# State products of an RWKV-7 mixer on the array's diagonal quarters, with states kept packed

## The reference

```
S_t = S_{t-1} (diag(w_t) - kk_t (kk_t*a_t)^T) + v_t k_t^T ;  y_t = S_t r_t
```

## Time and profile before

| | |
|---|---|
| median of 3 runs | 1588.71 us (1586.63 to 1590.48) |
| the profiled execution's own time | 1587.97 us |
| its span | 1586.0 us |
| mean granted TensorE clock | 0.923 |
| PE busy | 1433.5 us (90%) |
| DVE busy | 982.6 us (62%) |
| ACT busy | 661.4 us (42%) |

### The profile page before, as it was taken

One profiled execution on the slowest core, in us unless ns is written; L12 is line 12 of the kernel. 1 busy time (PEld: TensorE's weight loads), 2 busy tenths in 40 slices (PEclk: granted clock), 3 DMA queues, 4 the chain that ended last, 5 costly groups with the idle time before them and its releaser, 6 DMA issues.

```text
span 1586.0 us, 27551 instructions
## 1 busy us (share of the span) xinstructions
PE 1433.5 (90%) x10889; PEld 1282.0 (81%) x10889; DVE 982.6 (62%) x1316; ACT 661.4 (42%) x745; POOL 152.6 (10%) x117
## 2 busy tenths in 40 slices
PE   5799799688879787999997999996999999999996
PEld 3688544367868557999997998994999999999996
DVE  0565643636546536455375567575788888888786
ACT  1354123321203113443323043334677677667763
POOL 0000133000000000000363002250000000000000
PEclk9899999788968688999998999996999999999996
DMA  7565799442050322434432533352788888888882
GB/s 271 207 240 207 282 386 381 184 177 69 40 213 2 137 80 80 148 143 167 176 136 69 220 133 97 130 193 80 288 298 298 303 321 302 304 322 297 303 310 106
DMA packets 49005, 321.17 MB, mean 203 GB/s; under 512 B 6080, under 2 KB 6224, under 8 KB 19936
## 3 DMA queue, kind: packets, MB, share of 16 engines
q1 hardware_dynamic: 41760, 292.53, 50.0%
q0 software_dynamic: 7168, 27.54, 4.7%
HBM read 315.66 MB, written 4.39 MB: 202 GB/s over the span
## 4 chain that ended last, share of the span: by engine, by line
PE 70%; issue 11%; DVE 9%; ACT 4%; DMA 4%; DVEq 1%; POOL 1%; POOLq 0%; ACTq 0%; SPq 0%
PE ps L335 33%; PE ps L2449 4%; PE ps L2451 4%; PE ps L2450 4%; PE ps L1616 3%; DMA ring<-in_w_mod 2%; PE ps L2400 2%; PE ps L493 2%; PE ps L347 2%; PE ps L725 1%; ACT wexp L324 1%; PE ps L1622 1%; PE ps L1103 1%; PE ps L1064 1%; PE ps L1081 1%
## 5 line engine op out<-in xcount | busy, mean ns | idle before, releaser
L2369 DVE TENSOR_TENSOR wexp<-ring,wexp 128x2816 fp32r<-128x2816 f32 x98 | 302.9, 3091 | 65.8 <-ACT wexp L324 65.7
L324 ACT ACTIVATE wexp<-ring 128x2816 fp32r<-128x2816 f32 x98 | 250.9, 2560 | 26.8 <-PE ps L2451 26.6
L335 PE MATMUL ps<-hx_hi,wsplit 128*128 128x320 f32 x1088 | 251.5, 315 | 4.4 <-DVE hx_lo L676 2.6
L335 PEld LDWEIGHTS ps<-hx_hi,wsplit 128*128 128x128 f32 x1088 | 186.3, 191 | 12.2 <-issue 11.3
L2449 PE MATMUL ps<-wexp,xg_hi 128*128 128x352 f32 x512 | 168.4, 329 | 2.7 <-DVE xg_lo L2585 2.7
L335 PE MATMUL ps<-hx_lo,wsplit 128*128 128x320 f32 x544 | 169.8, 312 | 0.0
L2451 PE MATMUL ps<-wexp,xg_lo 128*128 128x352 f32 x512 | 165.2, 323 | 0.0
L2450 PE MATMUL ps<-wexp,xg_hi 128*128 128x352 f32 x512 | 165.0, 322 | 0.0
L324 ACT ACTIVATE wsplit<-ring 128x2048 fp32r<-128x2048 f32 (+1 forms) x60 | 120.0, 2000 | 98.8 <-PE ps L335 67.2
L335 PE MATMUL ps<-wexp,he_hi 128*128 128x256 f32 x704 | 128.6, 285 | 0.0
L314 POOL TENSOR_TENSOR wsplit<-ring,wsplit 128x2048 fp32r<-128x2048 f32 (+1 forms) x16 | 85.5, 5346 | 340.4 <-ACT wsplit L324 340.4
(11 more groups left out here) (393 smaller groups left out, 2671.6 us busy)
## 6 DMA issues: line engine op xcount, KB each, us to landing
ring<-in_exp_w SPq DMA_DIRECT2D x100, 1408.0 KB, 7.0
ring<-in_w_mod SPq DMA_DIRECT2D x48, 1024.0 KB, 7.8
ring<-in_ffn_gu SPq DMA_DIRECT2D x22, 1024.0 KB, 4.8
arena<-in_cache_k SPq DMA_DIRECT2D x64, 256.0 KB, 6.0
arena<-in_cache_v POOLq DMA_DIRECT2D x64, 256.0 KB, 5.8
ring<-in_w_in_o SPq DMA_DIRECT2D x16, 1024.0 KB, 4.7
ring<-in_w_in_e SPq DMA_DIRECT2D x13, 1024.0 KB, 4.9
ring<-in_ffn_down SPq DMA_DIRECT2D x8, 1408.0 KB, 6.0
```

The costliest lines, as they stand in the source:

```text
L324: return nc.scalar.activation(out, in_, ACT.Copy)
L335: mm = nc.tensor.matmul(out, u, v, start=first and p == 0, stop=last and p == 2)
L2369: eng.tensor_tensor(lo, ring[:, expert_slot(j), :], hi.bitcast(F32), ALU.subtract).then_inc(lo_exp, 1)
```

## The change

States stay packed in `S9`, 64 rows for each head of a pair. The block matrices `ATm` and `Sbd` and their memsets are gone. A state product takes the head's 64 rows of the state and of the chunk's matrix and writes the head's 64 partitions, so that it lies on a 64x64 quarter on the array's diagonal. Chunks are taken in pairs (`PAIRS`): (0, 1) and (2, 3) in tiles 0 and 1, and (0, 2), (1, 3), (4, 6), (5, 7) in tile 2, two chunks of a pair always in different groups of 32 rows. `pair_products` alternates the two chunks matmul by matmul, and every pair writes banks 2 to 5; one ScalarE copy of 128x1024 takes all four banks to `AC`. The decay is no longer applied to each term but once to the sum. DVE's state update is add, add, multiply, on 256 columns in tiles 0 and 1 and on two chunks at once, 512 columns, in tile 2. In tiles 0 and 1 both pairs' products now stand ahead of step 0, and the turn of the next tile stands behind the wait for the third state.

```diff
--- before.py
+++ after.py
@@ -1175,12 +1175,10 @@
     gup = aR.take(512)
     st = aR.take(5, 4 * P)
     stR, stQ, stK, stB, stV = (st[:, n, :].rearrange("p (j t) -> p j t", t=P) for n in range(5))
-    ATm = aR.take(2, 512)
+    AC = [aR.take(4, 256)]
     S9 = aR.take(9, 256)
-    Cst = aR.take(2, 256)
-    Sbd = aR.take(2, 512)
-    T1 = aR.take(256)
-    T2 = aR.take(256)
+    AC.append(aR.take(4, 256))
+    Tst = aR.take(2, 256)
     RW = aR.take(4, P)
     Y0 = aR.take(4, P)
     tokK, tokB, tokV = (aR.take(512) for _ in range(3))
@@ -1306,8 +1304,6 @@
         nc.vector.tensor_tensor(tmpR[:, :, :], kk[:, :, :], kk[:, :, :], ALU.mult
                                 ).then_inc(rp["kk_sq"], 1)
         nc.vector.memset(S9[:, 0, :], 0.0)
-        nc.vector.memset(Sbd[:, :, :], 0.0)
-        nc.vector.memset(ATm[:, :, :], 0.0)
         dve.wait_ge(rp["sig"], 1)
         flat = "p j t -> p (j t)"
         for j in range(4):
@@ -1356,21 +1352,19 @@
     def both(*names):
         return [f"{x}{h}" for x in names for h in range(2)]
 
+    PAIRS = (((0, 1), (2, 3)), ((0, 2), (1, 3), (4, 6), (5, 7)))
+
...
-        def chunk_matrices(cc):
-            dve.wait_ge(r_pe, P_.at(f"wc{cc}"))
-            x = cc % 2
-            for q in (0, 64):
-                nc.vector.tensor_copy(heads4(ATm[q:q + 64, x, :])[:, :, q:q + 64],
-                                      heads4(ps[q:q + 64, 2 + 2 * x, :])[:, :, q:q + 64])
-            for q in (0, 64):
-                last = nc.vector.tensor_tensor(
-                    Cst[q:q + 64, x, :].rearrange("p (j v) -> p j v", v=64),
-                    heads4(ps[q:q + 64, 3 + 2 * x, :])[:, :, q:q + 64],
-                    pend[q:q + 64, :, cc:cc + 1].to_broadcast([64, 4, 64]), ALU.mult)
-            last.then_inc(r_dve, 1)
-
-        def chunk_state(cc):
-            s_ = state(part, cc)
-            pe4 = pend[:, :, cc:cc + 1].to_broadcast([P, 4, 64])
-            v4 = "p o (j v) -> p (o j) v"
-            nc.vector.tensor_tensor(T1.rearrange("p (j v) -> p j v", v=64), s_.rearrange(v4, v=64),
-                                    pe4, ALU.mult)
+        def new_states(step, s_, C_, decay, ps_):
+            n = s_.shape[1]
+            tmp = Tst[:, 0:n, :]
+            nc.vector.tensor_tensor(tmp, s_, C_, ALU.add)
             dve.drain()
-            nc.vector.tensor_tensor(T1, T1, Cst[:, cc % 2, :], ALU.add)
-            dve.wait_ge(r_pe, P_.at(f"y{cc}"))
-            nc.vector.tensor_tensor(T2.rearrange("p (j v) -> p j v", v=64),
-                                    ps[:, 6, 0:256].rearrange("p (j v) -> p j v", v=64), pe4,
-                                    ALU.mult)
+            dve.wait_ge(r_pe, P_.at(f"y{step}"))
+            nc.vector.tensor_tensor(tmp, tmp, ps_, ALU.add)
             dve.drain()
-            if part == 0 and cc < C - 1:
-
-                for q in (0, 64):
-                    h = slice(q, q + 64)
-                    last = nc.vector.tensor_tensor(
-                        heads4(Sbd[h, (cc + 1) % 2, :])[:, :, q:q + 64],
-                        *(x[h, :].rearrange("p (j v) -> p j v", v=64) for x in (T1, T2)), ALU.add)
-                last.then_inc(r_dve, 1)
-            last = nc.vector.tensor_tensor(s_, T1.unsqueeze(1), T2.unsqueeze(1), ALU.add)
-            if part or cc == C - 1:
-                last.then_inc(r_dve, 1)
+            nc.vector.tensor_tensor(s_.rearrange("p x (j v) -> p x j v", v=64),
+                                    tmp.rearrange("p x (j v) -> p x j v", v=64), decay, ALU.mult
+                                    ).then_inc(r_dve, 1)
             dve.drain()
-        chunk_matrices(0)
-        chunk_matrices(1)
-        chunk_state(0)
-        for cc in range(2, C):
-            chunk_matrices(cc)
-            chunk_state(cc - 1)
-        chunk_state(C - 1)
+        for p, (ca, cb) in enumerate(PAIRS[part]):
+            dve.wait_ge(r_act, A_.at(f"ac{p}"))
+            if part:
+                decay = pend[:, :, ca:cb + 1:2].rearrange("p j x -> p x j")
+                new_states(p, S9[:, ca + 1:cb + 2:2, :], AC[p % 2][:, 1:4:2, :],
+                           decay.unsqueeze(3).to_broadcast([P, 2, 4, 64]),
+                           ps[:, 6, :].rearrange("p (x n) -> p x n", x=2))
+            else:
+                for y, cc in enumerate((ca, cb)):
+                    decay = pend[:, :, cc:cc + 1].rearrange("p j x -> p x j")
+                    new_states(cc, S9[:, 0:1, :], AC[p % 2][:, 2 * y + 1:2 * y + 2, :],
+                               decay.unsqueeze(3).to_broadcast([P, 1, 4, 64]),
+                               ps[:, 6:7, 0:256])
         dve.wait_ge(r_act, A_.at("y0"))
         nc.vector.tensor_tensor(col(yT), stg(ps[:, 7, :].rearrange("p (j t) -> p j t", t=P)),
                                 stg(Y0), ALU.add).then_inc(r_dve, 1)
@@ -1576,17 +1546,11 @@
         act.wait_ge(r_pe, P_.at("yr"))
         nc.scalar.activation(Y0[:, :, :].rearrange("p j t -> p (j t)"), ps[:, 0, :], ACT.Copy
                              ).then_inc(r_act, 1)
-        if t and part == 0:
-            act.wait_ge(r_dve, rdve[t - 1].at(f"s{n_chunks(0) - 1}"))
-        for cc in range(n_chunks(part) if part else 1):
-            if cc > 1:
-                act.wait_ge(r_pe, P_.at(f"y{cc - 2}"))
-            s_ = state(part, cc)
-            for q in (0, 64):
-                last = nc.scalar.activation(
-                    Sbd[q:q + 64, cc % 2, :].rearrange("p (o j v) -> p o j v", o=1, v=P)[:, :, :, q:q + 64],
-                    s_[q:q + 64, :, :].rearrange("p o (j v) -> p o j v", v=64), ACT.Copy)
-            last.then_inc(r_act, 1)
+        for p in range(len(PAIRS[part])):
+            act.wait_ge(r_pe, P_.at(f"wc{p}"))
+            if p >= 2:
+                act.wait_ge(r_dve, D_.at(f"s{p - 2}"))
+            nc.scalar.activation(AC[p % 2][:, :, :], ps[:, 2:6, 0:256], ACT.Copy).then_inc(r_act, 1)
 
     def turn_tensor(pe, t):
         pe.wait_ge(r_prod, t + 1)
@@ -1703,59 +1667,70 @@
                                    stop=True)
         last.then_inc(r_pe, 1)
 
-        def chunk_products(cc):
-            x = cc % 2
-            if part:
-                if cc == 0:
-                    pe.wait_ge(r_act, A_.at("masked"))
-                r = slice(RC * (cc // 2), RC * (cc // 2) + RC)
-                Bs, Ks = mats[x]["ET"], mats[x]["MT"]
-            else:
-                r = slice(RC * cc, RC * cc + RC)
-                Bs, Ks = tokB, tokK
+        def pair_products(p):
+            if p:
+                pe.wait_ge(r_act, A_.at(f"ac{p - 1}"))
+            elif part:
+                pe.wait_ge(r_act, A_.at("masked"))
             for j in range(4):
                 for n in range(3):
-                    for h in range(2):
-                        q = 64 * h
-                        own = slice(j * P + q, j * P + q + 64)
-                        U, W = (ZF[r, 2 * P * j + y + q:2 * P * j + y + q + 64] for y in (0, P))
-                        B, K, V = (y[r, own] for y in (Bs, Ks, tokV))
-                        a_, c_ = (ps[q:q + 64, y + 2 * x, own] for y in (2, 3))
-                        if n == 0:
-                            mm_(a_, W, B, start=True, stop=True)
-                        elif n == 1:
-                            mm_(c_, K, V, start=True, stop=False)
+                    for y, cc in enumerate(PAIRS[part][p]):
+                        if part:
+                            r = slice(RC * (cc // 2), RC * (cc // 2) + RC)
+                            Bs, Ks = mats[cc % 2]["ET"], mats[cc % 2]["MT"]
                         else:
-                            last = mm_(c_, B, U, start=False, stop=True)
+                            r = slice(RC * cc, RC * cc + RC)
+                            Bs, Ks = tokB, tokK
+                        for h in range(2):
+                            q = 64 * h
+                            own = slice(j * P + q, j * P + q + 64)
+                            U, W = (ZF[r, 2 * P * j + z + q:2 * P * j + z + q + 64] for z in (0, P))
+                            B, K, V = (z[r, own] for z in (Bs, Ks, tokV))
+                            a_, c_ = (ps[q:q + 64, z + 2 * y, 64 * j:64 * j + 64] for z in (2, 3))
+                            if n == 0:
+                                mm_(a_, W, B, start=True, stop=True)
+                            elif n == 1:
+                                mm_(c_, K, V, start=True, stop=False)
+                            else:
+                                last = mm_(c_, B, U, start=False, stop=True)
             last.then_inc(r_pe, 1)
 
-        def chunk_step(cc):
-            pe.wait_ge(r_dve, D_.at(f"ac{cc}"))
-            if cc:
-                pe.wait_ge(r_dve, D_.at(f"s{cc - 1}"))
-            if part or cc == 0:
-                pe.wait_ge(r_act, A_.at(f"bd{cc}"))
-            for j in range(4):
-                for q in (0, 64):
-                    mm_(ps[q:q + 64, 6, j * 64:j * 64 + 64],
```

(65 more changed lines are left out.)

## The result

The changed kernel takes 1579.57 us (median of 15 runs, 1571.64 to 1586.73) against 1589.77 (15 runs, 1586.43 to 1595.75): a ratio of 0.9924, 95% interval 0.9908 to 0.9941, so 0.76% or 12 us faster; the medians themselves lie 10.2 us apart. The forecast was 1578.3, in a range of 1565 to 1592.

The account below looks back on a forecast made before the run. TensorE, at half clock most of the time, bounds three stretches of 73.64 us, all on the path. Tiles 0 and 1 together -0.3, tile 2 -10.1, sum -10.4: 1577.6, or 1578.3 beside the median; range 1565 to 1592.

Parts of the forecast that it names:

- PE is in order: Reason why the three tile stretches are on the path: the next unit's matmuls stand right behind, so savings reach the end.
- (c): Pair products: two chunks in different 32-row groups run side by side, 1.92 us a pair at full clock, 2.76 at half.
- (a): Two memsets on DVE go; they were hidden behind a wait for ScalarE's sigmoid, so worth 0.
- (b): One ScalarE copy per pair, 1.03 us; PE waits for it between pair 0 and pair 1, a hole of 1.28 us a tile.
- B: Rival: row groups don't overlap in the pair products, which cost as now; sum +6.1 us, 1595; chance 0.16.
- (d): State products on 64x64 diagonal quarters keep the old pace: 1.05 us a chunk at full clock, 1.85 at half.
- C: Rival: two row halves in one bank take turns; each of 16 steps costs 1.6 us more, 1604; chance 0.05.
- (e): DVE's state chain, 0.93 us on 256 columns, is now exposed in tiles 0 and 1; a period is 2.97 us at half clock.
- (f): The next tile's turn now stands behind the wait for s2; the price, 1.07 us, is inside the third period of (e).
- The clock: TensorE's clock falls to 0.50 some 3.8, 4.0 and 5.8 us into tiles 0, 1, 2, returning near the turn's end.
- A: Rival: the clock stays high in all three tiles; sum -25.6 us, 1563; chance 0.09.
- A fully busy PE left at half: Reason against A: from 508 to 512 PE is busy 4.00 of 4.00 us with small tiles, still at 0.50.

Follow-up runs that it names:

- single row group: Changed kernel with tile 2's pairs reading the same 32 rows, still alternating: 1587.00 us, 0.9978 of the kernel before.
- two experiments: Changed kernel with a pair's chunks issued one after the other, 1.0050 of the kernel before; and with tile 2's pairs sharing 32 rows, 0.9978.
- holes filled: Changed kernel with unread full-array matmuls where PE idles (10 between pairs, 6 or 8 ahead of state waits): 1565.90 us, 0.9838 of the kernel before.
- covered, two banks: Changed kernel with pair 1 behind step 0, the turn ahead of the third-state wait, and two state banks in tile 2: 1568.61 us, 0.9848 of the kernel before.
- chain covered: Changed kernel with, in tiles 0 and 1, pair 1 behind step 0 and the turn ahead of the third-state wait: 1570.18 us, 0.9884 of the kernel before.
- before, filled: Kernel before the change with unread full-array matmuls ahead of state steps (4 at first and last, 7 between): 1584.94 us, 0.9958 of the kernel before.

## Why the prediction came out right

- The three stretches are all on the path, and what is saved reaches the end: 11.1 us in the stretches, 11.3 in the span, the last 0.2 by luck as said above. "PE is in order", which the prediction gave as a reason, is not so for single instructions (368.79 before 368.90 in the earlier trace rows), which its part (c) had seen itself.
- (a) Memsets at 0: nothing of them is seen, but no run tried them alone.
- (b) The hole: pair 1 starts 498.49 - 495.72 = 2.77 us after pair 0 in tile 2. Of this 12 groups at 0.117 us are 1.4, and 1.37 is the hole (forecast 1.28), with 1.02 for the copy (forecast 1.03).
- (c) The pair: at half clock 2.76 us, to the hundredth. At full clock 1.4 instead of 1.92: the floor of 20 ns that I took from the narrowest attention instructions does not hold here (14.6 ns), and the lower bound was the truth. It cost the forecast 0.5 us in each pair that ran at full clock, and two other errors covered it. In tile 1 the prediction's own terms give 2.4 us for pair 1 (0.8 us of it at full clock), not the 2.0 that it adds; measured were 436.01 - 434.06 = 1.95. In tile 2 the clock fell 4.6 us in instead of the 5.8 carried over from the earlier trace rows, and took back what the pairs gave: 25.52 against 25.6. So each stretch is nearer to its forecast than the terms were. The Trainium skill's rule that matmuls start in program order ("TensorE: Matmul & The Clock Gate", "Part 3: Packing small matmuls — row/col tiling") does not describe these traces: L1712 at 379.51 starts before L1706 at 379.61, as 368.79 lies before 368.90 in the earlier trace rows. B put a pair at half clock at 5.4 us, which is what the single row group took (5.3); the change took 2.76. B is refuted by that and by two experiments.
- (d) The step: 377.50 - 375.53 = 1.97 us to the start of DVE's read at half clock, as forecast, the old pace: 16 of the 64x64 instructions start within 0.91 us, as 16 of 128x64 did before. C, with 1.6 us more a step, is refuted: the quarters do overlap in one bank. What turns would cost was not measured.
- (e), (f) A period 3.02 (forecast 2.97), and three gaps of 1.1. That tiles 0 and 1 would give back what pairs saved was the step on which the sum turned, and covering the chain gave 2.7 us a tile.
- The clock: it fell and returned about where I had left it, so the sum held. That is luck in part, as the runs with the same code in tile 1 show (9.3 us at full clock in two of them). And my reason against A was weak. "A fully busy PE left at half" speaks of a clock that is to come back; it says nothing on whether one that is up can be held. With the holes filled it was held, with 16.1 us for tiles 0 and 1 by too many fillers and 11.8 with fewer and the covered order. A as I wrote it (the clock would stay by itself) did not come about in the change's traces, but it is not excluded: without a filler the clock stayed up through all of tile 2 in the run covered, two banks, and until 509.6 in the run chain covered. That its condition can be made likely is what the study adds: in the profiles of the four packed kernels with fillers it was 1.00 through all eight stretches of tiles 0 and 1, and in those of the eight without fillers through none of sixteen. The spread of 15 us among the changed kernel's 15 runs, against 9 before, fits this, as the moment of the fall differs; no run isolates that.

## What to carry to other kernels

In this kernel two matmuls of 32 rows cost the time of one when they read different row groups and stand next to each other in the order of issue: choose the pairs, then alternate them. When products are made cheaper, look at once at what they covered: here a chain of 1.1 us became visible six times, and moving one pair and the turn hid it again four times. And price a stretch of small matmuls at both granted clocks: in tiles 0 and 1 the covered order is worth 15.7 or 11.8 us a tile, and a few wasted matmuls in a hole that is there anyway went with the lower figure each time.

## What was not expected of the hardware

Fillers in a hole of 1.4 us went with a granted clock of 1.00 through stretches of 11.7 us, where in the same order without them it fell to 0.50 within 4 us in all four, while a PE busy 2.00 of 2.00 us on 32x64 and 64x64 tiles stayed at 0.50. What decides is not settled: the clock also stayed up with the hole empty (9.3 us of tile 1 in two runs, all of tile 2 in one) and fell once while PE was busy throughout and ran fillers (438.8 in the run before, filled). And PE started instructions of different row groups out of their order of issue (L1712 at 379.51 before L1706 at 379.61), so that an edit meant to end the overlap of two row halves cost only 0.54 us a step.
